# Recurrent rounds of a two-block model on one core: another order of the instruction streams

## What is computed

```
def _rwkv_scan(state, ins, emit):
    def step(S, inp):
        w_t, k_t, v_t, kk_t, a_t = inp[:5]
        sa = einsum('bhvk,bhk->bhv', S, kk_t)
        S = S * w_t - sa * (kk_t * a_t) + v_t * k_t
        y = einsum('bhvk,bhk->bhv', S, inp[5]) if emit else None
        return S, y

decay = exp(-exp(w_log));  a = sigmoid(a0[d] + xa @ a_up[d])
kk = k * k_k;  kk = kk * rsqrt(sum(kk * kk) + 1e-12);  k_mod = k * (1 + (a - 1) * k_a)
bonus = sum(r * k_mod * r_k[d]) * v
```

## Time and profile before

| | us |
|---|---|
| median of 3 runs (1707.97 to 1709.66) | 1708.23 |
| the profiled execution's own time | 1706.29 |
| its span, first to last instruction | 1704.5 |
| TensorE busy in the span | 1614.3 (95%) |
| VectorE busy / ScalarE busy | 462.7 / 336.4 |

### The profile page before, as it was taken

One profiled execution on the slowest core, in us unless ns is written; L12 is line 12 of the kernel. 1 busy time (PEld: TensorE's weight loads), 2 busy tenths in 40 slices (PEclk: granted clock), 3 DMA queues, 4 the chain that ended last, 5 costly groups with the idle time before them and its releaser, 6 DMA issues.

```text
span 1704.5 us, 25917 instructions
## 1 busy us (share of the span) xinstructions
PE 1614.3 (95%) x11539; PEld 1277.4 (75%) x11539; DVE 462.7 (27%) x1043; ACT 336.4 (20%) x704; POOL 19.3 (1%) x33
## 2 busy tenths in 40 slices
PE   6999967979799899999999999999999999999998
PEld 1545455868688687777788888888777878888887
DVE  1331033564743313223332100001412433200001
ACT  1200053343522302033400000001103430000000
POOL 2000001000000000000000000000000000000000
PEclk9999988989899999999999999999999999999999
DMA  9422200000002524423333444453443324344440
GB/s 366 165 99 74 66 34 1 3 2 4 17 3 100 126 99 148 148 99 113 127 125 131 153 156 157 159 142 103 145 148 104 143 99 148 129 158 157 150 161 25
DMA packets 110862, 191.27 MB, mean 112 GB/s; under 512 B 20872, under 2 KB 27280, under 8 KB 110624
## 3 DMA queue, kind: packets, MB, share of 16 engines
q1 hardware_dynamic: 109216, 186.20, 31.7%
q10 hardware_dynamic: 576, 2.11, 0.3%
q0 software_dynamic: 960, 1.33, 0.2%
HBM read 188.57 MB, written 1.05 MB: 111 GB/s over the span
## 4 chain that ended last, share of the span: by engine, by line
PE 78%; issue 16%; DVE 2%; ACT 1%; POOL 1%; DVEq 1%; POOLq 0%; ACTq 0%
PE psum L1064 28%; PE psum L1208 13%; PE psum L1149 9%; PE psum L786 5%; PE psum L1072 4%; PE psum L711 3%; PE psum L1232 2%; PE psum L947 1%; PE psum L1135 1%; PE psum L1178 1%; PE psum L702 1%; PE psum L1091 1%; PE psum L967 1%; PE psum L870 1%; ACT arena L1671 1%
## 5 line engine op out<-in xcount | busy, mean ns | idle before, releaser
L1064 PE MATMUL psum<-arena 128*128 128x256 f32 x2208 | 480.6, 378 | 0.0
L1064 PEld LDWEIGHTS psum<-arena 128*128 128x128 f32 x2208 | 417.4, 189 | 61.7 <-issue 1.3
L1671 ACT ACTIVATE arena<-psum 128x512 f32<-128x512 f32 (+6 forms) x230 | 119.9, 527 | 595.8 <-PE psum L1064 132.6
L1208 PE MATMUL psum<-arena 128*128 128x256 f32 x1024 | 222.2, 378 | 0.0
L1208 PEld LDWEIGHTS psum<-arena 128*128 128x128 f32 x1024 | 193.6, 189 | 28.3
L1149 PE MATMUL psum<-arena 128*128 128x256 f32 x768 | 176.5, 382 | 0.0
L1149 PEld LDWEIGHTS psum<-arena 128*128 128x128 f32 x768 | 141.8, 189 | 26.6 <-issue 5.3
L1287 PE MATMUL psum<-arena 128*128 128x512 f32 (+1 forms) x368 | 140.1, 538 | 2.0 <-issue 1.3
L1287 PEld LDWEIGHTS psum<-arena 128*128 128x128 f32 x368 | 68.7, 189 | 72.6 <-issue 68.0
L786 PE MATMUL psum<-arena 64*64 64x64 f32 x3072 | 96.3, 219 | 1.4 <-issue 1.4
L786 PEld LDWEIGHTS psum<-arena 64*64 64x64 f32 x3072 | 92.5, 134 | 6.6 <-issue 4.4
(11 more groups left out here) (312 smaller groups left out, 1267.4 us busy)
## 6 DMA issues: line engine op xcount, KB each, us to landing
arena<-in_w_in SPq DMA_DIRECT2D x33, 2048.0 KB, 7.7
arena<-in_w_up SPq DMA_DIRECT2D x16, 2048.0 KB, 7.6
arena<-in_w_down SPq DMA_DIRECT2D x16, 2048.0 KB, 7.8
arena<-in_mod_w SPq DMA_DIRECT2D x6, 2048.0 KB, 12.9
arena<-in_w_out SPq DMA_DIRECT2D x6, 2048.0 KB, 7.9
arena<-in_w_branch SPq DMA_DIRECT2D x6, 2048.0 KB, 8.4
arena<-in_w_in SPq DMA_DIRECT2D x3, 1024.0 KB, 6.8
arena<-in_w_in SPq DMA_DIRECT2D x12, 256.0 KB, 4.7
```

Of the source, the lines that this page charges most:

```text
L1064: mm = pe.matmul(b[:, i * T:(i + 1) * T], w[:, k, c:c + P], src[:, k, :], start=k == 0, stop=k == ks - 1)
L1208: mm = pe.matmul(bs[t][:, 0:T], w[:, k, t * P:(t + 1) * P], hff[:, c * KT + k, :], start=c == 0 and k == 0, stop=c == 3 and k == KT - 1)
L1671: return act.activation(dst, src, ACT.Copy, scale=scale)
```

## The change

The list of turns is written anew, two streams are cut more finely, and nothing is computed differently:

- The full score products L0 to L3 stand behind the first four inverse steps (`ILHILHILHILH`); before, they were spread over six.
- The preparation E begins two inverse steps earlier, at I4. Its step with `Ln` (E4) stands before I10 now and was behind it. Its last four steps (the decays' exponentials and the keys) stand among the chain steps C0 to C4; before, the first stood before C0.
- The decays are four steps and were two: for each direction ScalarE makes its `sw` and `pl` exponentials in one and its `cl` exponentials in the next; on VectorE, the first product of the keys is cut off into the earlier of the two. The bonus comes two steps later in E's count.
- In the third round, Q and N are spread over the last six inverse steps; their last ones (Q5, N5) stand behind I11 now and stood before it.

```
-TAIL = "TETETEETEEHEHTEHEHTHETH"
+TAIL = "TETETEETEEHEHTEHEHETEHETH"
...
-        turns += list("SSS" + "ILHIHILHIHILHIHL")
+        turns += list("SSS" + "ILHILHILHILH")
...
-            turns += list(f"IEQ{n}IEQ{n}IEQ{n}IEIEQ{n}EQ{n}IEQ{n}" + "CECHCHECHCHECHCHC" + "Y")
+            turns += list("IEHIEH" + f"IEQ{n}IEQ{n}IQ{n}IEQ{n}IEQ{n}IQ{n}" + "CECEHCEHCEHCHCHECHCE" + "Y")
...
-            turns += list("IQNIQNIQNIQNQNIQNIM" + "CMCMCMCMCMCMCMCM" + "YMNNMNMNNMMMMN")
+            turns += list("IHIH" + "IQNIQNIQNIQNIQNIQNM" + "CMCMCMCMCMCMCMCM" + "YMNNMNMNNMMMMN")
...
-            for _ in range(6):
+            for _ in range(8):
                 yield
             pe.wait_ge(sem("e_bonus"), j + 1)
...
                 act.activation(ecol[:, j % 2, d], ecol[:, j % 2, d], ACT.Exp)
                 act.drain()
+                yield
                 for c in range(4):
                     q = slice(c * P, (c + 1) * P)
                     act.activation(cl[:, d, q], cl[:, d, q], ACT.Exp, scale=DECAY, bias=nmid[:, d, c:c + 1])
...
                 dve.tensor_tensor(la[:, d, :], kn, la[:, d, :], ALU.mult)
+                yield
                 dve.wait_ge(sem("e_decays"), 2 * j + d + 1)
```

## The result

| | before | after |
|---|---|---|
| median of the runs, us | 1708.52 (20 runs, 1705.81 to 1710.92) | 1713.00 (20 runs, 1708.22 to 1718.39) |
| profiled execution, us | 1706.29 | 1717.10 |
| its span, us | 1704.5 | 1715.3 |
| its mean granted clock | 0.979 | 0.973 |
| TensorE busy in it, for the same 11539 instructions | 1614.3 | 1628.9 |

The ratio is 1.0026, 95% interval 1.0016 to 1.0037: slower by 4.5 us. The forecast had 1707.7, "no change", and the median stands on the upper edge of its range. It was wrong in its direction: -0.5 forecast, +4.5 measured. The executions also lie further apart: 10 us after, 5 us before.

A forecast was written before the change was run, and what follows sets the result against it. TensorE was taken as the bound through its waits, two of them queues on VectorE and ScalarE. Terms -0.9, -2.2, -2.4 and +5.0 gave -0.5 us: 1705.8 profiled, 1707.7 median, range 1703.0 to 1713.0.

The forecast's parts named there:

- Part 1, the opening: Before the first round: H3 comes 2.0 us earlier, the bonus product costs 1.1 behind T5; -0.9 us.
- Part 2: Inverse with L and E moved: no cost except a 2.4 us wait before N2's product in round two; +1.2 us.
- Part 3, the key norm: Before C1, rounds one and two: Exp 2.6 and 3.2 us earlier; waits of some 3.2 and 1.1 us remain.
- Part 4, the chains: From Exp on in rounds one and two: the earlier start mostly stays, despite new short waits; -2.2 and -2.4 us.
- from C0 to Y 34.1 us before, some 30.5 after: Sign to look for: the stretch from L855's first eight products to L896's first row shortens this much.
- 0.8 us for the low clock in the chains: First round's chain: TensorE makes `s` of C1 at the half clock after its idle time; +0.8 us.
- The rival that had this mechanism: Both rounds' chains: several short waits keep the clock at 1.2 GHz; 1714.9 us, or 1711 with half; chance 0.20.
- The third rival: Chains of rounds one and two: VectorE is late for `x6` for another reason, no gain; 1713.5 us; chance 0.08.
- Part 5, the third round: At M0: an added wait of 3.2 us and a low clock of 1.8 behind it; +5.0 us.
- the 0.15 us for the semaphore: Third round, before M0: 0.15 us added to VectorE's finish at 534.15, putting M0's start at 534.3.
- The row of the Trainium skill: ScalarE's table switch at about 2.66 us; if right, 1.4 us more gain in each round, 1704.9; chance 0.02.

The follow-up runs named there:

- e2: The kernel before with only the third round's order changed: Q5 and N5 behind I11; 1714.09 us, ratio 1.0037.
- e7: The kernel before plus 28 unread products on TensorE in the waits before L870 in the first two rounds; 1708.94 us, ratio 1.0001.
- e8: The kernel before with one move alone: E4 (table load and Ln of the key norm), with Q3 and N3, before I10; 1704.77 us, ratio 0.9978.
- e13: The kernel after, unchanged, profiled and run a second time; 1712.44 us, ratio 1.0025.
- e4: The kernel after with the cumulation step E3 moved behind L2026, before I9; 1710.06 us, ratio 1.0013.
- e9: The kernel after with 7 unread products in place of the longest wait before C1 in rounds 1 and 2; 1711.30 us, ratio 1.0014.
- e5, the two repairs: The kernel after with Q5 and N5 before I11 in the third round and E3 behind L2026; 1702.89 us, ratio 0.9965.
- e11: The kernel after with 7 unread products before C1 and 3 before the diagonal products, rounds 1 and 2; 1710.55 us, ratio 1.0009.
- e1: The kernel after with Q5 and N5 before I11 again in the third round; 1705.60 us, ratio 0.9989.

## Why the prediction was wrong, step by step

- **Part 1, the opening (-0.9).** T3 to C0 of round 1 is 107.2, 108.0, 108.3 and 108.5 us in the four profiles of kernels with the opening of before (before, e2, e7, e8). Of the thirteen with the new one ten are 105.6 to 106.6 and three 108.5 to 108.7 (e13 is one). So it gains some 1.3 us on average and 2 in most. The sign and the size are right, and no experiment has it alone.
- **Part 2 (+1.2).** N2's wait is 2.56 us instead of the 2.4 forecast. The mechanism is right (e4 takes it away by moving the step). What was left out of the sum, as if it were nothing, is the clock behind it: L786's group takes 4.69 us in the kernel after, 6.03 in e9 and 3.77 in e13. By the runs of e4 and e5 the step's place costs 2.2 to 4.1 us and not 1.2.
- **Part 3, the key norm.** `Exp` 1.3 us behind I10's copies, waits of 3.14 and 0.51 where 3.2 and 1.1 were forecast. The second is short because the products before it run at the low clock and fill it: 1.09 + 0.51, and in e13's second round, where they take 0.63 us, 0.63 + 0.96. The mechanism is right, and by e8 worth -3.8 us by itself.
- **Part 4, the chains (-2.2 and -2.4).** This step failed: "from C0 to Y 34.1 us before, some 30.5 after". It was 36.62 and 33.71 in one execution of the kernel, 31.60 and 30.67 in another. The waits at C1 were right and the later ones shorter than forecast, so in a good execution the forecast came true, to 1.0 us in the first round (30.6 by its -2.2, 31.60 measured) and to 0.2 in the second. In most of the profiled ones it did not in the first chain (five of six), since the sum had only 0.8 us for the low clock in the chains, and that in the first round. The first chain pays 5 us in those, and the second 3 in two of six. The rival that had this mechanism (several short waits keep the clock at 1.2 GHz) got a chance of 0.20, and its argument against, that "slow products fill the gap before `diag`", was wrong in an instructive way: the gap before `diag` was indeed shorter than foreseen (1.44 for 2.5), and the clock stayed low all the same. That rival also had this in both rounds and in each execution, which the runs don't show; it was right in place and kind. Its time was added up wrongly: 1707.7 + 7.7 is 1715.4, not 1714.9, and with half of it 1711.6, not 1711. The median lies between the two. The third rival's 1713.5 is nearest to the median, by luck: its mechanism, that VectorE is late for `x6` for another reason and the chains gain nothing, is refuted by the waits at C1.
- **Part 5, the third round (+5.0).** The wait is 3.30 (3.2 forecast), the low clock 1.4 (1.8). By runs it is 6.3 us (e2, 3.9 to 8.7). No row here shows the 0.15 us for the semaphore as a term of its own; the wait it is part of came out right. The term held; 1.5 us more lie behind C0 of round 3 in e2's profile (1173.08 for 1171.53), but other profiles vary there by as much.
- **The sum by runs:** parts 1 to 4 brought -1.9 in place of -5.5, part 5 +6.3 in place of +5.0. The two errors, 3.6 and 1.3, make the 5 us between forecast and measurement. For the first the runs point to the low clock that the sum left out, behind the short waits of the chains and behind N2's wait: with the chains' waits filled (e11) 2.9 us come back, and with N2's taken away 2.2 to 4.1. How the 3.6 us divide between the two they are too coarse to show.
- The row of the Trainium skill on ScalarE: Activation LUTs (What ACT_TABLE_LOAD costs, some 2.66 us for a switch) was weighed in the forecast and the measured 1.29 taken. In the kernel after `Exp` starts at 343.77 behind a load at 342.47, 1.30 us, so the trace again disagrees with the page.

What stays open: why the clock comes back at 362.5 us in one execution and at some 374.5 in another of the same program, with the same waits. Also whether the half clock comes in the unprofiled runs as often as in the profiled ones. And why the chains' gain in the profiles with fillers, 5 to 6 us in the first, comes to 1.7 to 2.9 us in the runs. The clock also falls after the rounds, and not at the same place in each execution. With TensorE busy for 40 us of 40, the kernel after shows this,

```profile
600.00:640.00 40.00, 39.98 (x183) 33.52 (x183) 11.22 (x29) 5.75 (x12) 0.00 (x0) 0.92 0.26 92
640.00:680.00 40.00, 40.00 (x178) 32.15 (x177) 10.97 (x20) 6.56 (x10) 0.00 (x0) 0.91 0.34 119
```

where the kernel before has 0.91 in the first window and 1.00 in the second.

## What to carry to other kernels

A wait that is cut into several short ones is not worth their difference. Look first at the duration of a known group of products behind each of them, and put the low clock into the sum for every one, above all where two follow each other closely. Where one move of a change could bring all of the gain by itself (here the key norm, -3.8 us alone) and others add waits, run it alone. And before a stage of a profile is compared with another, profile one of the two kernels a second time: here the same program differs by 8.7 us between two executions, twice the effect that was to be explained.

## What the runs showed of the hardware that I had not expected

- Work that nobody reads, put where TensorE waits, can make the kernel faster: with 45 such products the ratio went from 1.0026 to 1.0003 (1713.00 to 1708.28 us), clear of the noise, and with ten in each of two rounds to 1.0009, just within it. On top of the two repairs it is not shown beyond the noise: 0.9965 without, 0.9963 and 0.9944 with (6, 5 and 5 runs).
- The granted clock stayed at 0.50 for a window of 10 us in which TensorE was 9.27 us busy (the kernel after, 360 to 370), and was 0.91 over 40 us in which it never paused (600 to 640 in the kernel before, 640 to 680 in the kernel after).
- One float32 product of 128x128 by 128x256 is two records of 0.23 us each: seven fillers are 14 records and 3.24 us.
- A stall of TensorE that no semaphore ends (named "issue", in the third round; 1.45 us in before and in e2, 1.2 in e8) is not there in the kernel after, in e1 and in e5. Nothing of the change aims at it.
